# Copies of the transposed cache keys: shared between ScalarE and VectorE by token half, with a semaphore for each engine

## What is computed

```python
past_k = cache_k[l][page_table].reshape(nb_s, n_pages * PAGE_SIZE, MOBA_HEADS, MOBA_HD)
past_v = cache_v[l][page_table].reshape(nb_s, n_pages * PAGE_SIZE, MOBA_HEADS, MOBA_HD)
...
gate = jnp.einsum('bqhd,bjhd->bhqj', qq.astype(jnp.float32), k_mean)
gate = jnp.where(blk_ids[None, None, None, :] < own[None, None, :, None], gate, -jnp.inf)
_, top = lax.top_k(gate, n_sel)
...
logits = jnp.einsum('bqhd,bhqsnd->bqhsn', qq, kg).astype(jnp.float32) * scale
logits = jnp.where(mask, logits, -jnp.inf).reshape(B, H, qc, -1)
p = jax.nn.softmax(logits, axis=-1).reshape(mask.shape).astype(v.dtype)
return jnp.einsum('bhqsn,bhqsnd->bqhd', p, vg)
```

## Time and profile before

| | before |
|---|---|
| median of three runs | 1565.12 us |
| profiled execution: its own time | 1564.92 us |
| span of its instructions | 1563.2 us |
| mean granted TensorE clock | 0.972 |
| TensorE busy | 1486.0 us, 95% |
| VectorE busy | 619.2 us, 40% |
| ScalarE busy | 256.0 us, 16% |

### The profile page before, as it was taken

One profiled execution on the slowest core, in us unless ns is written; L12 is line 12 of the kernel. 1 busy time (PEld: TensorE's weight loads), 2 busy tenths in 40 slices (PEclk: granted clock), 3 DMA queues, 4 the chain that ended last, 5 costly groups with the idle time before them and its releaser, 6 DMA issues.

```text
span 1563.2 us, 19813 instructions
## 1 busy us (share of the span) xinstructions
PE 1486.0 (95%) x7506; PEld 663.2 (42%) x7506; DVE 619.2 (40%) x1221; ACT 256.0 (16%) x518; POOL 35.2 (2%) x70
## 2 busy tenths in 40 slices
PE   6899998999898989999999999999999999999995
PEld 2554564576676655333333333333333333333331
DVE  3106535311444346442442443443443443443435
ACT  1112021144564013100100100100000000000001
POOL 0000000000123000000000000000000000000000
PEclk9999998699899989999999999999999999999998
DMA  9533459363787747799999999999999999999992
GB/s 335 211 108 108 155 213 336 117 236 88 211 283 253 269 138 308 288 424 427 429 428 429 429 429 428 429 428 428 428 428 429 429 428 429 428 427 429 428 429 102
DMA packets 76864, 515.16 MB, mean 330 GB/s; under 512 B 8241, under 2 KB 17015, under 8 KB 49168
## 3 DMA queue, kind: packets, MB, share of 16 engines
q1 hardware_dynamic: 71696, 497.73, 78.3%
q0 software_dynamic: 5120, 16.78, 3.2%
HBM read 507.14 MB, written 7.34 MB: 329 GB/s over the span
## 4 chain that ended last, share of the span: by engine, by line
PE 90%; DVE 3%; DMA 3%; ACT 2%; issue 1%; SPq 1%; DVEq 0%; ACTq 0%
PE ps L1015 28%; PE ps L1034 14%; PE ps L1043 6%; PE ps L904 6%; PE ps L988 6%; PE ps L552 5%; PE ps L615 5%; PE ps L778 5%; PE ps L640 4%; PE ps L1004 2%; DMA ring<-in_w_ada 1%; PE ps L750 1%; DMA ring<-in_w_proj_gla 1%; PE ps L587 1%; PE ps L643 1%
## 5 line engine op out<-in xcount | busy, mean ns | idle before, releaser
L1015 PE MATMUL ps<-ring,mem 128*64 128x512 f32 x2048 | 446.5, 594 | 0.7 <-ACT mem L1299 0.7
L1015 PEld LDWEIGHTS ps<-ring,mem 128*64 128x64 f32 x2048 | 144.3, 137 | 300.1 <-issue 299.2
L1034 PE MATMUL ps<-ring,mem 128*64 128x512 f32 x1024 | 227.1, 596 | 0.0
L1852 DVE TENSOR_SCALAR mem<-ps 128x512 f32<-128x512 f32 x32 | 22.2, 692 | 370.5 <-PE ps L1015 370.5
L1869 DVE TENSOR_TENSOR mem<-ps,mem 128x1024 f32<-128x1024 f32 (+1 forms) x99 | 121.0, 1222 | 54.7 <-PE ps L1043 51.3
L1034 PEld LDWEIGHTS ps<-ring,mem 128*64 128x64 f32 x1024 | 70.8, 137 | 153.2 <-issue 153.2
L1871 DVE TENSOR_TENSOR mem<-mem 128x1024 f32<-128x1024 f32 (+1 forms) x99 | 121.1, 1224 | 3.4
L1043 PE MATMUL ps<-mem 64*128 64x512 f32 (+1 forms) x396 | 110.9, 637 | 2.7 <-DVE mem L1869 1.4
L552 PE MATMUL ps<-mem 128*128 128x128 f32 (+2 forms) x495 | 89.9, 310 | 20.5 <-ACT mem L1265 11.0
L1303 ACT ACTIVATE mem<-mem 128x512 f32<-128x512 f32 x32 | 20.2, 632 | 511.2 <-DVE mem L1852 511.2
L552 PEld LDWEIGHTS ps<-mem 128*128 128x128 f32 (+2 forms) x495 | 65.7, 182 | 85.9 <-issue 59.4
(11 more groups left out here) (305 smaller groups left out, 1127.4 us busy)
## 6 DMA issues: line engine op xcount, KB each, us to landing
ring<-in_w_gate_up SPq DMA_DIRECT2D x128, 2048.0 KB, 15.5
ring<-in_w_down SPq DMA_DIRECT2D x64, 2048.0 KB, 14.2
ring<-in_w_in SPq DMA_DIRECT2D x13, 2048.0 KB, 12.4
ring<-in_w_ada SPq DMA_DIRECT2D x12, 2048.0 KB, 9.5
ring<-in_cache_k SPq DMA_DIRECT2D x64, 256.0 KB, 3.4
ring<-in_cache_v POOLq DMA_DIRECT2D x64, 256.0 KB, 4.4
ring<-in_state_gla SPq DMA_DIRECT2D x2, 2048.0 KB, 10.6
out<-ring SPq DMA_DIRECT2D x2, 2048.0 KB, 8.1
```

What stands on the lines that cost most here:

```text
L1015: last = mm(out, xeT[:, 2 * (s % 2) + k, s // 2, :], w[:, k, 512 * q:512 * q + 512], start=False, stop=s == 3 and k == 1)
L1034: last = mm(ps[64 * f:64 * f + 64, 0, :], actT[:, k, s, :], w[:, k, 512 * f:512 * f + 512], start=s == 0 and k == 0, stop=s == 1 and k == 3)
```

## The change

The four groups of token half 0 (jj = 0, 2, 4, 6, banks 0 and 2) stay with ScalarE and count in `kt2_a`. The four of half 1 (jj = 1, 3, 5, 7, banks 1 and 3) go to VectorE and count in `kt2_d`. Each engine waits for its own group alone. TensorE waits for both counters ahead of the scores and ahead of `cache_probs`, and for the one that emptied the bank within `cache_keys`. The copy of a tile itself is the same operation with the same shape.

```diff
@@ TensorE @@
                 for jj in range(2 * PAIRS):
                     p, f = divmod(jj, 2)
                     if jj >= 4:
-                        pe.wait_ge(kt2_sb, b * 8 + jj - 3)
+                        pe.wait_ge(kt2_d if f else kt2_a, b * 4 + p - 1)
...
             def cache_scores(b):
 
-                pe.wait_ge(kt2_sb, b * 8 + 8)
+                pe.wait_ge(kt2_a, b * 4 + 4)
+                pe.wait_ge(kt2_d, b * 4 + 4)
                 pe.wait_ge(q_sb, b + 1)
...
             def cache_probs(b, keys_before):
 
-                pe.wait_ge(kt2_sb, keys_before)
+                pe.wait_ge(kt2_a, keys_before)
+                pe.wait_ge(kt2_d, keys_before)
                 pe.wait_ge(cs_exp, b + 1)
...
-            cache_probs(0, 15)
+            cache_probs(0, 8)
...
-                cache_probs(b, b * 8 + 15)
+                cache_probs(b, b * 4 + 8)
@@ ScalarE @@
             def cache_keys(b):
-                for jj in range(8):
-                    act.wait_ge(kt2_ps, b * 8 + jj + 1)
-                    f = jj % 2
-                    a.copy(kTs[:, jj // 2, 512 * f:512 * f + 512], ps[:, jj % 4, :]).then_inc(kt2_sb, 1)
+                for p in range(PAIRS):
+                    act.wait_ge(kt2_ps, b * 8 + 2 * p + 1)
+                    a.copy(kTs[:, p, 0:512], ps[:, 2 * (p % 2), :]).then_inc(kt2_a, 1)
@@ VectorE @@
+            def cache_keys(b):
+                for p in range(PAIRS):
+                    dve.wait_ge(kt2_ps, b * 8 + 2 * p + 2)
+                    v.tensor_copy(kTs[:, p, 512:1024], ps[:, 2 * (p % 2) + 1, :]).then_inc(kt2_d, 1)
...
             queries(0)
+            cache_keys(0)
             cache_max(0)
             queries(1)
+            cache_keys(1)
             cache_probs(0)
             for b in range(1, NB - 1):
                 cache_max(b)
                 if b <= 4:
                     projected(b - 1)
                 queries(b + 1)
+                cache_keys(b + 1)
                 cache_scale(b - 1)
                 cache_probs(b)
                 cache_out(b - 1)
```

More of the change, by code:

```diff
@@ L326, in decoder_layer @@
             sem(n) for n in ("ms_ps", "ms_max", "ms_exp", "mt_ps", "mt_sb", "mo_ps", "mo_sb", "mot_ps", "mot_sb"))
-        q_sb, kt2_ps, kt2_sb, cs_ps, cs_max, cs_exp, cp_ps, cp_a, cp_d, co_ps, co_sb, cot_ps, cot_sb = (
-            sem(n) for n in ("q_sb", "kt2_ps", "kt2_sb", "cs_ps", "cs_max", "cs_exp", "cp_ps", "cp_a", "cp_d",
+        q_sb, kt2_ps, kt2_a, kt2_d, cs_ps, cs_max, cs_exp, cp_ps, cp_a, cp_d, co_ps, co_sb, cot_ps, cot_sb = (
+            sem(n) for n in ("q_sb", "kt2_ps", "kt2_a", "kt2_d", "cs_ps", "cs_max", "cs_exp", "cp_ps", "cp_a", "cp_d",
                              "co_ps", "co_sb", "cot_ps", "cot_sb"))
@@ L932, in _ @@
             pe.wait_ge(pj_sb, 7)
-            cache_probs(NB - 1, NB * 8)
+            cache_probs(NB - 1, NB * 4)
             cache_out(NB - 2)
```

## The result

| | before | after |
|---|---|---|
| median of the runs at first | 1565.02 us (7 runs, 1557.2 to 1566.74) | 1575.50 us (7 runs, 1570.06 to 1575.59) |
| ratio | 1 | 1.0063, interval 1.0049 to 1.0077 |
| repeated on another occasion | 1566.02 us (26 runs, 1560.03 to 1571.27) | 1574.03 us (9 runs, 1568.10 to 1575.94) |
| ratio then | 1 | 1.0045, interval 1.0031 to 1.0059 |
| profiled execution, its own time | 1564.92 us | 1570.06 us |

Both comparisons say slower by over 0.2%: +9.9 and +7.0 us as ratios of 1566. I forecast slower, +4.5 us, 1566.5 to 1572.0. The direction was right, the size was not. The profiled execution of the changed kernel happens to be the fastest of its seven, so 1570.06 us must not be taken for its usual time.

What follows compares the result with a forecast made beforehand. TensorE, busy 95% of the span, was taken to bound the kernel, other engines mattering only where it waits. Stalls +6.85, gain -2.4, weights wait -1.95, clock +2.0 gave +4.5 us on 1564.92: 1569.4 us, range 1566.5 to 1572.0.

Steps and rivals of the forecast that it cites:

- which wait ends last: Turns 0, 5, 6: VectorE reaches its first key copy only behind its maxima, so TensorE waits about 3.4 us.
- stalls in turns 0, 5 and 6, clock kept up: Key transposes wait for VectorE, exponentials start later: +2.35 us in turn 5, +2.25 in turns 6 and 0, together +6.85.
- gain in turns 1 to 4: Behind the projection, exponentials start some 0.6 us earlier each turn: -2.4 us, bounds 0 and -4.7.
- wait for the weights swallowed: End of the cache stage: TensorE's 1.96 us wait for projection weights absorbs part of the delay, -1.95 us.
- clock in turns 5 and 6: TensorE's clock falls in each new 3.4 us wait, priced at 2 x 0.8 = 1.6 us.
- clock in turn 0, with what reaches turn 1: Turn 0 already has a clock fall; the waiting splits over two gaps, +0.4 us, between -1.2 and +1.6.
- my sum without the clock: Stalls, gain and swallowed weights wait together, TensorE's clock left out: +2.5 us.
- In turn 0 the fall is there already ... which I price at +0.4: Turn 0's waiting splits over two gaps and ends nearer busy work: +0.4 us, between -1.2 (no fall) and +1.6.
- a fall costs between 0 and 1.6 us of the path ... I take half: Turns 5 and 6: part of a slow stretch is spent waiting, so each clock fall costs 0.8 us.
- every stall brings a full fall: Rival: turns 0, 5 and 6 each pay 1.6 us of clock, +7.3 in all, 1572.2 us; chance 0.13.
- what the sum was made against: Baseline 1564.92 us, the profiled execution, 0.2 us below the median of three runs; +4.5 gives 1569.4 us.
- The clock stays up: Rival: TensorE keeps 2.4 GHz through the stalls, 1567.4 us, or 1566.2 if turn 0 loses its fall; chance 0.20.

Runs made afterwards that it cites:

- the turns at the edges alone: Changed kernel with VectorE sharing key copies only in turns 0, 5 and 6, ScalarE's loop split; 1578.92 us, ratio 1.0078 to the kernel before.
- the middle alone: Changed kernel with VectorE sharing key copies only in turns 1 to 4, ScalarE's loop split; 1566.32 us, ratio 0.9994 to the kernel before.
- the two fed kernels: The kernel before and the changed kernel, each with extra TensorE transposes, read by nobody, in its waits; 1563.96 and 1570.44 us.
- fed changed kernel: Changed kernel plus unread transposes: 24 before group 5 in turns 0, 5, 6, 16 before turn 0's probabilities, 48 behind the last projections; 1570.44 us, ratio 1.0022.
- fed kernel before: Kernel before plus unread transposes: 28 ahead of turn 0's probabilities and 48 in the wait behind the last projections; 1563.96 us, ratio 0.9985.
- filled kernel: Changed kernel plus 24 unread transposes ahead of group 5 of the key transposes in turns 0, 5 and 6; 1569.34 us, ratio 1.0016.

## Why the prediction was wrong, point by point

**Right: which wait ends last.** Turns 0, 5 and 6 have no projection, and VectorE reaches its first copy only behind its maxima. TensorE's waits of 3.46 us (turn 0) and twice 3.36 us were forecast at about 3.4 us. The two halves of the change show it: the turns at the edges alone carry the whole loss, the middle alone loses nothing.

**The terms of the sum, against the stage.** The clock-free sizes are from the two fed kernels, turn by turn, the rest from the first traces of the plain ones. The clock is what is left.

| us | forecast | measured |
|---|---|---|
| stalls in turns 0, 5 and 6, clock kept up | +6.85 | +7.85 |
| gain in turns 1 to 4 | -2.4 | -3.15 |
| wait for the weights swallowed | -1.95 | -2.02 |
| clock in turns 5 and 6 | +1.6 | +1.9 |
| clock in turn 0, with what reaches turn 1 | +0.4 | +1.56 |
| sum | +4.5 | +6.14 |

**Right, with a size a little off: the gain in turns 1 to 4.** Forecast 0.6 us each; turns 2 to 4 gave 0.79. The exponentials start 0.72 us earlier, since group 6 was ready earlier than my pace of 0.46 us a group had it, and from their start to TensorE's it also takes less (434.45 to 436.86 is 2.41 us, 435.15 to 437.63 was 2.48).

**Right, with a size a little off: the stalls without the clock.** In the fed changed kernel turns 0, 5 and 6 took 12.96, 12.98 and 12.97 us, 7.85 us over the fed kernel before, where I had 6.85. TensorE resumed when I said, 7.74 us after the start of turn 5's scores in the filled kernel; from there to the exponentials it took 1.61 us, where I had 1.32. This error and that of the gain nearly cancel: without any fall the stage is +2.1 us, and my sum without the clock said +2.5. That the two agree is in part luck.

**The step that failed: "In turn 0 the fall is there already ... which I price at +0.4".** Measured, turns 0 and 1 lose 2.87 us to the clock after the change (14.82 and 14.77 us, against 12.96 and 13.76 in the fed kernel) and 1.31 us before it (11.31 and 14.89, against 10.34 and 14.55). The difference is 1.56 us, at the upper end of the -1.2 to +1.6 that I had given. The fall did not stay what it was. It grew from some 3 us to some 10 us, since the one wait of 3.5 us became one of 3.46 and another of 2.08 us behind it, and nearly all the work between and behind them ran at half speed. The same turn before is not a constant: with turn 1 it took 26.20, 27.67 and 26.35 us in the three traces, 29.59 and 29.57 after.

The other part of the term, "a fall costs between 0 and 1.6 us of the path ... I take half", held: 1.04 us in turn 5 and 0.87 in turn 6 (changed kernel less filled kernel), where I had 0.8 each. The low stretch began while TensorE still waited, and the slow transposes used up the old 1.34 us wait for the exponentials. The rival "every stall brings a full fall" had 1.6 us for each and was too high in turns 5 and 6. In turn 0 it had 1.6 and measured 1.56, so there it was right.

**The second part of the miss: what the sum was made against.** I took 1564.92 us, one execution, and the median of three runs. Later runs of the same kernel lie between 1559 and 1572 us, with a median of 1566.02 over 26. Against that, my sum says 1570.5, and the repeated measurement is 1574.0, 3.5 us more. The stage explains 1.6 us of this, or 1.8 against the mean of three traces of before. Behind the stage the traces differ by 1.1 us, most of it chance, and what is then left, under 1 us, is within the uncertainty of either comparison. The first comparison, 9.9 us, lies 2 to 3 us above all this; no trace shows where, and it stays open.

**The range.** I built it from one trace's terms and did not put in that the same program moves by 11 us from run to run. "The clock stays up" with 1566.2 to 1567.4 was out: the clock fell in turns 0, 5 and 6 in both traces. In the filled kernel, where it stays up in turns 5 and 6, the ratio is 1.0016, 2.5 us, which is near that rival's number.

## What to carry to other kernels

An engine that is idle on average can be busy at the one moment when it is wanted: before moving work to it, look at what stands in front of the work on its list in each pass of the loop, and split the loop where the answer differs. Here the same sharing gains 0.8 us behind a projection and costs 2.6 us without one, and 3.5 to 3.7 us with the clock. A new wait of TensorE needs a price for the slow work behind it: here 0.9 to 1.0 us for a wait that stood alone, and 2.9 us where a second wait followed. A baseline should be several runs with their granted clocks before 0.2% is argued over, and a trace should be compared stretch by stretch, since its other stretches can be short or long by more than the change. And an edit that only splits a loop can move a table load onto the path, 1.2 us here.

## What the runs showed of the hardware that was not expected

- More work on TensorE can make a kernel faster: 72 idle transposes brought 1574.0 to 1569.3 us, by filling waits of 3.4 us. The stage became 3.4 us shorter.
- The same program on one core spreads by 11 us (1560.03 to 1571.27 over 26 runs), and the mean granted clock goes with it on the whole (0.976 for the shortest, 0.970 and 0.967 for the two longest, though 0.973 for one of 1569.02).
- Two turns with equal rows up to the last wait (1.40 us, 1.53 us of work, 2.49 us) ended at different clocks, 10 transposes in 1.29 and in 2.37 us.
- The same loop of ScalarE, split in three, loads its function table at another place: 1.28 us ahead of turn 0's exponentials in place of ahead of the copies, and turn 0 is 1.2 us longer.
- This one was expected, and held: ScalarE and VectorE copied 128x512 tiles out of different banks side by side at 0.59 and 0.69 us each, as they do alone.
